# Fused kernel of a hybrid attention model on one Trainium2 core: modulation sums, panel splits, pooling and attention units in a new order

## What is computed

```python
def hybrid_layer(x, mod, ...):
    shift1, scale1, gate1, shift2, scale2, gate2 = jnp.split(mod[:, None, :], 6, axis=-1)
    h = rms_norm(x, norm1) * (1.0 + scale1) + shift1
    proj = h @ w_in                      # u (512 columns), q (512), k and v, gates
    y_pool = pool_mixer(u, pool_w, pool_scale)
    y_nsa = nsa_mixer(q, kv[:, :, 0], kv[:, :, 1], gates, ...)
    mix = jnp.concatenate([y_pool, y_nsa], axis=-1) @ w_out
    x = x + gate1 * mix
    h2 = rms_norm(x, norm2) * (1.0 + scale2) + shift2
    ff = jnp.square(jax.nn.relu(h2 @ w_ff1)) @ w_ff2
    return x + gate2 * ff

for l in range(DEPTH):                   # DEPTH is 2
    mod = c_act @ w_mod[l] + b_mod[l]    # one row of 1024 times 1024 x 6144
    x = hybrid_layer(x, mod, ...)
```

## Time and profile before

| | us |
|---|---|
| median of 3 runs | 1372.97 |
| lowest and highest | 1372.44 and 1376.41 |
| the profiled execution's own time | 1375.51 |
| its span in the trace | 1373.7 |
| busy in the span: PE / DVE / ACT / POOL | 1278.3 / 938.7 / 621.0 / 38.5 |
| mean granted clock of PE | 0.939 |

### The profile page before, as it was taken

One profiled execution on the slowest core, in us unless ns is written; L12 is line 12 of the kernel. 1 busy time (PEld: TensorE's weight loads), 2 busy tenths in 40 slices (PEclk: granted clock), 3 DMA queues, 4 the chain that ended last, 5 costly groups with the idle time before them and its releaser, 6 DMA issues.

```text
span 1373.7 us, 21734 instructions
## 1 busy us (share of the span) xinstructions
PE 1278.3 (93%) x8834; PEld 1169.2 (85%) x8834; DVE 938.7 (68%) x1223; ACT 621.0 (45%) x828; POOL 38.5 (3%) x42
## 2 busy tenths in 40 slices
PE   6599999999999999899999999998889998999997
PEld 6587897999989778799999998787669987899996
DVE  5778766887857696775557559987874663755553
ACT  2444225444444522444443535468775632644432
POOL 1001200000000130000000000000000000000000
PEclk8699589999998977999999999999989999899998
DMA  9534533776655163465555542355754451555530
GB/s 377 204 143 154 184 123 136 296 282 264 244 197 193 53 219 125 189 215 183 183 183 220 208 178 93 116 178 200 230 172 151 154 184 61 185 190 185 186 142 31
DMA packets 43621, 247.69 MB, mean 180 GB/s; under 512 B 4160, under 2 KB 12368, under 8 KB 15520
## 3 DMA queue, kind: packets, MB, share of 16 engines
q1 hardware_dynamic: 43104, 244.57, 49.4%
q0 software_dynamic: 448, 2.14, 0.4%
HBM read 245.58 MB, written 1.11 MB: 180 GB/s over the span
## 4 chain that ended last, share of the span: by engine, by line
PE 70%; DVE 17%; DMA 6%; ACT 5%; issue 2%; SPq 0%; POOL 0%; DVEq 0%; ACTq 0%
PE bank L386 14%; PE bank L388 13%; PE bank L387 13%; PE bank L682 12%; PE bank L683 6%; DVE w_lo L381 4%; DVE arena L1010 3%; PE bank L802 2%; ACT w_hi L376 2%; DMA arena<-in_modw 2%; DVE arena L1905 1%; DMA arena<-dscr 1%; DMA raw<-in_panels 1%; PE bank L761 1%; DMA mixf<-dscr 1%
## 5 line engine op out<-in xcount | busy, mean ns | idle before, releaser
L381 DVE TENSOR_TENSOR w_lo<-raw,w_hi 128x2048 fp32r<-128x2048 f32 x170 | 388.8, 2290 | 190.7 <-ACT w_hi L376 190.1
L376 ACT ACTIVATE w_hi<-raw 128x2048 fp32r<-128x2048 f32 x170 | 324.2, 1910 | 228.8 <-DMA raw<-in_panels 115.3
L682 PE MATMUL bank<-act,w_hi 128*128 128x512 f32 x768 | 281.0, 407 | 11.5 <-DVE act L1031 5.5
L386 PE MATMUL bank<-act,w_hi 128*128 128x256 f32 x800 | 238.1, 298 | 8.9 <-DVE act L1031 7.4
L386 PE MATMUL bank<-ff_hi,w_hi 128*128 128x256 f32 (+1 forms) x816 | 230.3, 282 | 1.9 <-issue 1.0
L388 PE MATMUL bank<-ff_hi,w_lo 128*128 128x256 f32 (+1 forms) x816 | 230.8, 283 | 0.0
L387 PE MATMUL bank<-ff_lo,w_hi 128*128 128x256 f32 (+1 forms) x816 | 230.7, 283 | 0.0
L387 PE MATMUL bank<-act,w_hi 128*128 128x256 f32 x800 | 230.4, 288 | 0.0
L388 PE MATMUL bank<-act,w_lo 128*128 128x256 f32 x800 | 230.3, 288 | 0.0
L683 PE MATMUL bank<-act,w_lo 128*128 128x256 f32 x768 | 218.2, 284 | 0.0
L682 PEld LDWEIGHTS bank<-act,w_hi 128*128 128x128 f32 x768 | 146.6, 191 | 51.0 <-issue 11.3
(11 more groups left out here) (320 smaller groups left out, 1786.8 us busy)
## 6 DMA issues: line engine op xcount, KB each, us to landing
raw<-in_panels SPq DMA_DIRECT2D x170, 1024.0 KB, 4.9
arena<-in_modw SPq DMA_DIRECT2D x48, 1024.0 KB, 6.8
mixf<-dscr SPq DMA_DIRECT2D x8, 512.0 KB, 5.9
arena<-dscr SPq DMA_DIRECT2D x8, 512.0 KB, 4.8
mixf<-dscr SPq DMA_DIRECT2D x8, 256.0 KB, 6.3
arena<-dscr SPq DMA_DIRECT2D x8, 256.0 KB, 5.3
cst<-in_cst SPq DMA_DIRECT2D x1, 1251.5 KB, 7.8
arena<-in_x SPq DMA_DIRECT2D x1, 1024.0 KB, 5.2
```

The lines of the kernel that those rows point to most:

```text
L376: nc.scalar.activation(w_hi[slot(k)][:, :], raw[:, k % RAW, :], ACT.Copy).then_inc(hi_done, 1)
L381: nc.vector.tensor_tensor(w_lo[slot(k)][:, :], raw[:, k % RAW, :], w_hi[slot(k)][:, :].bitcast(F32), ALU.subtract).then_inc(lo_done, 1)
L386: nc.tensor.matmul(o, wh, xh, start=start, stop=False, skip_group_check=skip)
L682: nc.tensor.matmul(bank[4 + c][:, :], wh[:, s:s + P], act2[:, kc, :, :], start=kc == 0, stop=False)
```

## The change

No arithmetic is left out or added. On **DVE** the sums 2 and 3 stand in the Q stage: 2 after the lo split of panel 6, 3 after the compressed keys' activation. Sums 4 and 5 follow the second query stack, all seven maxima of group 1 follow one another, sum 6 stands behind weigh 1. The lo splits of panels 9, 10 and 11 stand later. On **ACT** the second `stack` is ahead of group 0's bounds, u is copied and announced in two parts, and the hi split of panel 11 stands behind `mixed(1)`. On **POOL** the pooling is done in two parts: groups 0 and 1 after U0, groups 2 and 3 after U1. On **PE** mod(1) and mod(2) stand inside panels U0 and U1, mod(3) between output steps, and PV units, scores, turns and output steps alternate one by one. **SP**'s loads are in the order that goes with it.

```diff
@@ sp_layer
             load_mod(sp, l, 8)
             load_mod(sp, l, 9)
-            for k in (4, 5, 6):
-                load(sp, m, k)
+            load(sp, m, 4)
+            load(sp, m, 5)
             load_mod(sp, l, 10)
+            load(sp, m, 6)
             load(sp, m, 7)
+            load_mod(sp, l, 11)
             load(sp, m, 8)
-            load_mod(sp, l, 11)
-            for k in (9, 10, 11):
-                load(sp, m, k)
             load_mod(sp, l, 12)
             load_mod(sp, l, 13)
+            load(sp, m, 9)
+            load(sp, m, 10)
             load_mod(sp, l, 14)
+            load_mod(sp, l, 15)
+            load(sp, m, 11)
+            load_mod(sp, l, 16)
             load(sp, m, 12)
-            load_mod(sp, l, 15)
+            load_mod(sp, l, 17)
             load(sp, m, 13)
-            for u in (16, 17, 18):
-                load_mod(sp, l, u)
+            load_mod(sp, l, 18)
             load(sp, m, 14)
@@ pool_window
+            pool.wait_ge(u_copied, 2 * l + 1)
+            link(tt(cols(b, 0, 2), cols(ub, 0, 2), cols(ub, 0, 2, 1), ALU.add))
+            link(tt(cols(c, 1, 2), cols(b, 1, 2), cols(b, 1, 2, 2), ALU.add))
+            for g, t in ((0, b), (1, c)):
+                link(tt(cols(t, g, g + 1), cols(t, g, g + 1), rc[:, g:g + 1, :], ALU.mult))
+                last = tt(cols(t, g, g + 1), cols(t, g, g + 1), cols(ub, g, g + 1), ALU.subtract)
+            last.then_inc(pooled_ready, 1)
             pool.wait_ge(u_copied, 2 * l + 2)
...
@@ pe_layer
             pe_maxima(pe, l, 0, 6)
+            mod(1)
             part(L_U0, 6, 12, 16)
...
             part(L_U1, 7, 8, 10)
+            pe.wait_ge(modc_ready, 3 * l + 2)
+            mod(2)
+            part(L_U1, 7, 10, 12)
             pe_maxima(pe, l, 1, 4)
             pe_maxima(pe, l, 1, 5)
-            part(L_U1, 7, 10, 13)
+            part(L_U1, 7, 12, 14)
             pe_maxima(pe, l, 1, 6)
-            mod(1)
-            part(L_U1, 7, 13, 16)
+            part(L_U1, 7, 14, 16)
             pe_pv(pe, l, 0)
             pe_bounds(pe, l, 1)
             pe_pv(pe, l, 1)
             pe_scores(pe, l, 1, 0)
-            pe_scores(pe, l, 1, 1)
             pe_turn(pe, l, 0)
             pe_pv(pe, l, 2)
+            pe_scores(pe, l, 1, 1)
             pe_scores(pe, l, 1, 2)
-            pe_scores(pe, l, 1, 3)
             pe_turn(pe, l, 1)
-            pe.wait_ge(modc_ready, 3 * l + 2)
-            mod(2)
             pe_pv(pe, l, 3)
-            pe_scores(pe, l, 1, 4)
-            pe_scores(pe, l, 1, 5)
+            for u in range(3, 7):
+                pe_scores(pe, l, 1, u)
             pe_turn(pe, l, 2)
-            pe_scores(pe, l, 1, 6)
             pe_turn(pe, l, 3)
...
-            mod(3)
             pe_pv(pe, l, 4)
-            pe_pv(pe, l, 5)
...
             pe_out(pe, m, L_POOL, (0, 4))
+            pe_pv(pe, l, 5)
+            pe_out(pe, m, L_POOL, (4, 8))
+            mod(3)
             pe_pv(pe, l, 6)
-            pe_out(pe, m, L_POOL, (4, 8))
+            pe_out(pe, m, L_POOL, (8, 12))
             pe_turn(pe, l, 4)
             pe_pv(pe, l, 7)
-            pe_out(pe, m, L_POOL, (8, 12))
+            pe_used(pe, pe_out(pe, m, L_POOL, (12, 16)))
             pe_turn(pe, l, 5)
...
@@ act_layer
             split_hi(act, m, 9)
+            stack(1)
             bounds(0)
...
-            exponentials(0, range(1))
-            stack(1)
-            exponentials(0, range(1, 7))
+            exponentials(0, range(7))
...
-            split_hi(act, m, 11)
-            mixed(0)
-            exponentials(1, range(2, 6))
-            exponentials(1, range(6, 7))
-            mixed(1)
+            exponentials(1, range(2, 3))
+            mixed(0)
+            exponentials(1, range(3, 7))
+            mixed(1)
             split_hi(act, m, 11)
...
@@ dve_layer
             split_lo(dve, m, 6)
+            mod(2)
...
+            mod(3)
             rotated(0)
...
             stack(1)
+            mod(4)
             split_lo(dve, m, 8)
...
```

More of the change, by code:

```diff
@@ L398, in pool_window, with cols @@
         def pool_window(pool, l, link):
-            pool.wait_ge(u_copied, 2 * l + 2)
[L401 to L415, removed]
+            b, c = wb
+            def cols(t, g0, g1, off=0):
+                return t[:, g0:g1, 16 - off:16 - off + T]
+            rc = cst[:, C_RC:C_RC + 4 * T].rearrange("p (g t) -> p g t", g=4)
+            tt = nc.gpsimd.tensor_tensor
+            pool.wait_ge(u_copied, 2 * l + 1)
[5 more added lines that the diff above has]
+            last.then_inc(pooled_ready, 1)
+            pool.wait_ge(u_copied, 2 * l + 2)
+            link(tt(cols(b, 2, 4), cols(ub, 2, 4), cols(ub, 2, 4, 1), ALU.add))
+            link(tt(cols(c, 2, 4), cols(b, 2, 4), cols(b, 2, 4, 2), ALU.add))
+            link(tt(cols(b, 2, 4), cols(c, 2, 4), cols(c, 2, 4, 4), ALU.add))
+            link(tt(cols(c, 3, 4), cols(b, 3, 4), cols(b, 3, 4, 8), ALU.add))
+            for g, t in ((2, b), (3, c)):
+                link(tt(cols(t, g, g + 1), cols(t, g, g + 1), rc[:, g:g + 1, :], ALU.mult))
+                last = tt(cols(t, g, g + 1), cols(t, g, g + 1), cols(ub, g, g + 1), ALU.subtract)
             last.then_inc(pooled_ready, 1)
@@ L642, in pe_layer @@
             pe_out(pe, m, L_POOL, (0, 4))
+            pe_pv(pe, l, 5)
+            pe_out(pe, m, L_POOL, (4, 8))
+            mod(3)
             pe_pv(pe, l, 6)
-            pe_out(pe, m, L_POOL, (4, 8))
+            pe_out(pe, m, L_POOL, (8, 12))
             pe_turn(pe, l, 4)
             pe_pv(pe, l, 7)
-            pe_out(pe, m, L_POOL, (8, 12))
+            pe_used(pe, pe_out(pe, m, L_POOL, (12, 16)))
             pe_turn(pe, l, 5)
-            pe_used(pe, pe_out(pe, m, L_POOL, (12, 16)))
             pe_out(pe, m, L_POOL + 1, (0, 5))
             pe_turn(pe, l, 6)
+            pe_out(pe, m, L_POOL + 1, (5, 7))
             pe_turn(pe, l, 7)
-            pe_used(pe, pe_out(pe, m, L_POOL + 1, (5, 16)))
+            pe_used(pe, pe_out(pe, m, L_POOL + 1, (7, 16)))
             pe.wait_ge(mix_los, 4 * l + 4)
@@ L813, in pe_turn @@
             nc.tensor.transpose(bank[6][:, (un % 2) * P:(un % 2 + 1) * P], o_sum[un % 3], ident).then_inc(tr_full, 1)
-        ACT_LINKS = 4
+        ACT_LINKS = 5
         def rsqrt(link, o, src, scale, eps):
@@ L923, in act_layer @@
             split_hi(act, m, 9)
+            stack(1)
             bounds(0)
             used(L_U0)
-            nc.scalar.activation(ub[:, 0:2, 16:16 + T], two(G(6)[:, :]), ACT.Copy).then_inc(gfree[0], 1)
-            exponentials(0, range(1))
-            stack(1)
-            exponentials(0, range(1, 7))
+            link(nc.scalar.activation(ub[:, 0:2, 16:16 + T], two(G(6)[:, :]), ACT.Copy))
+            act.sem_inc(gfree[0], 1)
+            act.sem_inc(u_copied, 1)
+            exponentials(0, range(7))
             split_hi(act, m, 10)
@@ L1196, in dve_layer @@
             stack(1)
+            mod(4)
             split_lo(dve, m, 8)
[L1198 to L1204, removed]
+            dve_modc(dve, modc_ready, 3 * l + 2, 16, lc[:, LC_BM:LC_BM + 8], 12 * l + 5)
+            mod(5)
+            maxima(1, range(7))
             weigh(0)
             weigh(1)
-            mod(5)
-            dve_modc(dve, modc_ready, 3 * l + 2, 16, lc[:, LC_BM:LC_BM + 8], 12 * l + 5)
+            mod(6)
             weigh(2)
-            split_lo(dve, m, 11)
             weigh(3)
             mixed(0)
-            mod(6)
-            mod(7)
+            split_lo(dve, m, 9)
             mixed(1)
@@ L1222, in dve_layer @@
                     last.then_inc(gfree[g // 2], 1)
+            mod(7)
             weigh(4)
             weigh(5)
-            mod(8)
+            split_lo(dve, m, 10)
             weigh(6)
@@ L1228, in dve_layer @@
             weigh(7)
+            mod(8)
+            mixed(3)
+            split_lo(dve, m, 11)
+            mod(9)
             split_lo(dve, m, 12)
-            mixed(3)
-            mod(9)
             mod(10)
```

4 lines of the change are left out of this document (2 added, 2 removed).

## The result

The changed kernel takes 1383.12 us (median of 4 runs, 1382.06 to 1384.39) against 1372.70 us (4 runs, 1372.12 to 1376.41): a ratio of 1.006, with a 95% interval of 1.0035 to 1.0086. It is slower, by 0.6% (0.8% by the medians). The profiled execution took 1382.06 us, its span is 1379.9 us against 1373.7, so 6.2 us have to be found.

What follows compares the result with a forecast made beforehand. PE held 70% of the chain of waits. Layer changes of 0 and +2.9 us on the profiled 1375.5 gave 1378.4; less 2.5 for the median, 1375.9, rounded to 1376 us, range 1366 to 1389.

Steps and rivals of the forecast that it cites:

- the side given 0.41: Chance that the changed kernel is slower, made of the clock-fall rival and the upper edges of two other cases.
- The 1.54 goes: PE's wait of 1.54 us for DVE's modulation sum ahead of mod(1) vanishes, in both layers.
- sums 2 to 5 fit the idle places: Sums 2 and 3 fill DVE waits of 3.77 and 3.26 us; sums 4 and 5 are done near 124 instead of 148.
- PV 0 at 131.3: First layer: the first PV unit on PE starts at 131.3 us instead of 133.21.
- D: Rival: DVE's idle places are too short for sums 2 and 3; one us over gives 1378 us, chance 0.07.
- 1.5 us of loss on sum 6 beside GpSimd: Second pooling part on POOL slows DVE's sum 6 by 1.5 us, bounded by zero and 5.6.
- A: The forecast case: clock 1.00 through PV 0 to 3, 1376 us, chance 0.33.
- B: Rival: clock falls during PV 0, bounds and PV 1; one layer gives 1383 us, both 1390; chance 0.34.
- Chain through panel 11: Split 9, panel 11's load, its hi split and the pooling copies set PV 4 at 156.1; PE waits 8 us.
- The clock's rise "14 us on": After PE's wait ahead of PV 4 the clock is at 0.50 and rises 14 us later, as in the trace before.
- C: Rival: alternating PV and output steps brings the clock back 5 us on; 3.7 us less per layer, 1368.5 us; chance 0.26.
- Tail of 23.8 instead of 17.2: DVE's work behind turn 5 takes 23.8 us up to the first x update, against 17.2 before.

Runs made afterwards that it cites:

- copies first: The changed kernel with ACT's hi split of panel 11 moved behind its four pooling copies: 1356.40 us, ratio 0.986 to the kernel before.
- split 9 early: The changed kernel with VectorE's lo split of panel 9 moved from behind mixed 0 to ahead of weigh 0: 1369.12 us, ratio 0.9974 to the kernel before.

## Why the prediction was right and wrong

The forecast was 1376 in a range of 1366 to 1389; it is 1383.1, on the side given 0.41. The 7.1 us between them are of two kinds. For the profiled execution the sum was 1378.4 and it took 1382.06, 3.7 more: that is what the steps below explain. The rest, some 3.5, came from taking 2.5 off for the median, because the profiled execution of the kernel before lay 2.5 above its median; that of the changed kernel lies 1.1 below. One execution's place among the runs is no property of the kernel, so that term had no ground. By its steps:

- *The 1.54 goes, sums 2 to 5 fit the idle places, PV 0 at 131.3.* Right, and better: 129.98. D has fallen (waits of 1.14 and 0.23 were left over).
- *1.5 us of loss on sum 6 beside GpSimd, between 0 and 5.6.* It was 0.8 and another 0.5 on weigh 1's product, with 2.2 us more on sums 4 and 5 and split 8, which TensorE doesn't wait for. By the rule of the Trainium skill (SBUF — State Buffer, section Who interferes with whom) the two engines lock each other out for whole instructions. The trace agrees, instruction by instruction: the product of 134.33 ends with GpSimd's of 134.24. The 5 us that I had worked out from it did not come because I took the rule for GpSimd's whole part of 7.5 us. That part is eight instructions of 0.64 to 1.06 us, VectorE gets its turn between two of them, and only the last 2.3 us stood beside sum 6. With larger GpSimd instructions, pooling in one part, sum 6 lost 2.7.
- *A, the clock stays up in PV 0 to 3.* Right: 1.00 in the window. B's condition did not occur, and its time of 1383 came out for another reason. That is luck, not a reading.
- *Chain through panel 11, PV 4 at 156.1 behind a wait of 8.* Right: 154.03 and 6.67. Two runs each took a link out: with the copies first PV 4 came 5.2 us earlier, with split 9 early 4.2.
- ***The clock's rise "14 us on", so PV 4 to turn 5 takes 20.7.* This step failed**, in its size and in its kind. It took 16.6 in one layer and 26.2 in the other, and 14.5 where TensorE did not wait. I took one trace's rise for a constant. The mean of the two, 21.4, is near my number by accident; beside it, the second layer had no rise at all before turn 5. C's number, 17.0, came true in the first layer, but its mechanism is not shown: without the alternation the clock came back 9 and 17 us behind PV 4, with it 5 and 28, so behind a long wait it is not what brings it back. I had also misread the stretch of 165.4 to 179.0, which I took in B for PV units alone: two groups of four output steps stand in it, at 171.45 and 176.74, and the first of them did not raise the clock, which speaks against C too. The Trainium skill (Perfetto Trace Analysis, section Matmul Optimizations) wants matmuls back to back; the run with 15 matmuls in the gap agrees, with its 12 us. The fall at 513.50 in the kernel before, behind 21.97 us without a gap, does not.
- *Tail of 23.8 instead of 17.2.* Right: 24.4 in both layers, the DMA wait of 2 us in it. The x updates came 5.5 us earlier and 2.4 us later than foretold. Of the 5.5 the stretch behind PV 4 made 4.1 and PV 4 itself 2.1; in the second layer the stretch lost 5.5 and PV 4 gained 3.7. The tail took 0.6 more than foretold in both.
- *"What follows the x updates is unchanged."* Wrong, and unpriced: a late VectorE leaves TensorE idle for 4.5 us before the norm sums, and the low clock behind that costs 2.9 us in the first layer and 1.5 in the second (from x update to feed-forward: 14.84 and 13.35 against 11.89 and 11.88).

## What to carry to other kernels

Where a change shortens the work ahead of a wait, look at what stands directly ahead of the waited-for instruction on its own engine: a weight split that waited for a load, one place ahead of four small copies, turned a gain of 1.4% into a loss of 0.6%. Price a wait of TensorE not by its length but by its length plus the work behind it at half the clock, with a range from nothing to all of it. Take the forecast for the runs from medians, not from where one profiled execution happened to lie. And when a stage's end moves, check that what the next stage needs isn't queued behind work that only some later stage needs.

## What the runs showed of the hardware

In most places the lower clock (0.50, 1.2 GHz) came after a wait of TensorE: the stretch of PV 0 to 3 ran at 1.00 for 15.5 us without a wait ahead of it, where it was at 0.50 before, behind the wait of 1.54 us. After waits of 2.45, 6.5 and 8.4 us it fell every time. The length of a short wait doesn't decide alone: behind 0.98 us in "copies first" it stayed up in both layers, behind 0.96 and 0.80 us in the kernel before it fell in both, with other matmuls following, and once it fell without any wait (513.50 above). How long it stays down doesn't follow from TensorE's work: 3 to 24 us behind the same 2.45 us wait. Runs of that kernel scatter over 20 us (1361.4 to 1381.3), and the mean granted clock goes with it, 0.957 to 0.939, so one trace is one draw. Idle time filled with useless matmuls was repaid: 6.6 us of them, in each of two layers, gave 12 us.

A VectorE instruction with two SBUF inputs, beside GpSimd's pooling, was held until the GpSimd instruction that ran beside it was done, but not for the rest of the pooling: 0.66 us instead of 0.17, ending at 134.99 where GpSimd's ended at 134.97.
